# Key half of a KV compression by three products for even and odd chunks, with the turned rows copied whole to SBUF

## The reference, cut to what matters

```python
def compress_rows(rows, pe, w1, w2):          # once for keys, once for values
    ch = rows[:, :n_chunks * 16].reshape(B, n_chunks, 16, G, D)
    proj = jnp.einsum('bnsgd,psdh->pbngh', ch, w1)      # p = 0, 1: two taps
    h = proj[0, :, 0:n_blk] + bias[0]
    h = h + proj[1, :, 1:1 + n_blk] + bias[1]
    return jnp.einsum('bngh,hd->bngd', jax.nn.silu(h), w2)
```

## Time and profile before

| | us |
|---|---|
| timed, median of three runs | 2232.06 (2231.8, 2232.06, 2240.67) |
| span of the profiled execution | 2233.0 |
| paged steps of the stage, 370 to 971 | 601 |
| PE busy, whole span | 2092.5 |

### The profile page before, as it was taken

The page is one execution under the profiler, slowest core; times in us unless marked ns, Lnnn a source line. Parts: engine busy times, 40 slices in busy tenths (PEclk is TensorE's granted clock), DMA queues, the critical chain, the costliest instruction groups (busy, mean ns, idle before and its releaser), DMA issues. The chain is left out here.

```text
span 2233.0 us, 41102 instructions
## 1 busy us (share of the span) xinstructions
PE 2092.5 (94%) x16006; PEld 1877.4 (84%) x16006; DVE 1471.5 (66%) x3233; ACT 1004.9 (45%) x2112; POOL 607.8 (27%) x932
## 2 busy tenths in 40 slices
PE   6999999999999999996789898997999999999997
PEld 5999997777777777774678787777999999999997
DVE  4222225777776776786578687558688788765667
ACT  4114223655554664654367486325333333334334
POOL 0001003444443443431069596120111111110000
PEclk9999999999999999986879999998999999999999
DMA  4116565554654654658510011331332332365342
GB/s 128 57 57 186 191 224 168 194 196 163 201 171 133 212 167 149 177 137 276 191 52 8 8 48 48 108 109 41 101 114 75 101 116 77 97 239 193 118 165 97
DMA packets 217338, 295.53 MB, mean 132 GB/s; under 512 B 23474, under 2 KB 160914, under 8 KB 207762
## 3 DMA queue, kind: packets, MB, share of 16 engines
q1 hardware_dynamic: 199736, 191.64, 27.7%
q0 software_dynamic: 17408, 101.26, 13.0%
HBM read 217.12 MB, written 82.63 MB: 134 GB/s over the span
## 5 line engine op out<-in xcount | busy, mean ns | idle before, releaser
L3241 DVE TENSOR_TENSOR a_XTL<-cpt,a_XTH 64x256 fp32r<-64x256 f32 (+1 forms) x576 | 230.5, 400 | 87.9 <-ACT a_XTH L3126 79.5
L3126 ACT CAST a_XTH<-cpt 64x256 fp32r<-64x256 f32 (+1 forms) x576 | 201.4, 350 | 97.5 <-PE cpt L3350 85.3
L3365 PE MATMUL cph<-a_XTH,w1H 128*128 128x512 f32 x512 | 216.0, 422 | 0.0
L3365 PE MATMUL cph<-a_XTL,w1H 128*128 128x512 f32 x512 | 204.4, 399 | 0.0
L3365 PE MATMUL cph<-a_XTH,w1L 128*128 128x512 f32 x512 | 204.1, 399 | 0.0
L1558 POOL TENSOR_TENSOR C<-C,a_mt 128x264 f32<-128x264 f32 x66 | 69.0, 1064 | 404.9 <-ACT C L1643 269.9
L2077 PE MATMUL f<-a_slot,wd_slot 128*128 128x264 f32 x1176 | 148.2, 285 | 2.0 <-DVE a_slot L1887 1.4
L2077 PEld LDWEIGHTS f<-a_slot,wd_slot 128*128 128x128 f32 x1176 | 144.8, 188 | 3.0 <-issue 2.2
L2040 PE MATMUL f<-a_b,ring 128*128 128x264 f32 x1056 | 144.0, 286 | 3.3 <-DVE a_b L1783 2.7
L2040 PEld LDWEIGHTS f<-a_b,ring 128*128 128x128 f32 x1056 | 135.5, 190 | 3.8 <-issue 3.8
L492 PE MATMUL pj<-wH,xL 128*128 128x256 f32 (+2 forms) x464 | 130.9, 282 | 0.0
(11 more groups left out here) (582 smaller groups left out, 5560.7 us busy)
## 6 DMA issues: line engine op xcount, KB each, us to landing
a_slot<-a_T SPq DMA_DIRECT2D x20, 792.0 KB, 4.6
raw<-in_w_in POOLq DMA_DIRECT2D x12, 1024.0 KB
V<-v_s SPq DMA_DIRECT2D x6, 2048.0 KB, 10.3
v_s<-X SPq DMA_DIRECT2D x22, 512.0 KB, 6.0
raw<-in_w_gate SPq DMA_DIRECT2D x22, 512.0 KB, 5.2
raw_odd<-in_w_val SPq DMA_DIRECT2D x22, 512.0 KB, 6.1
a_T<-C SPq DMA_DIRECT2D x20, 528.0 KB, 3.3
a_T<-sums SPq DMA_DIRECT2D x11, 792.0 KB, 4.9
```

Of the source, the lines that this page charges most:

```text
L3126: nc.scalar.copy(turned(XTH, u, s, k, g, a), split(bank(at, k)[:], u, k, g, a)).then_inc(h_ready, 1)
L3241: last = nc.vector.tensor_tensor(turned(XTL, u, s, k, g, a), split(bank(at, k)[:], u, k, g, a), hi.bitcast(F32), ALU.subtract)
L3365: last = nc.tensor.matmul(out[:, :, 0:n], w[:, s, k, q, m * P:(m + 1) * P], x[:, s % 2, k, :, q:q + n], **flags)
```

## The change

For the key half, the 256 chunks are split in even ones E and odd ones O, 128 of each for each head. A block at an even position is w0·E + w1·O of the same pair, a block at an odd position w0·O + w1·E of the next pair. The kernel computes three products: w0·O and w1·E (kept apart in the banks `taps`), and (w0 + w1)·(E + O) in the bank `joint`; the even blocks are the joint product less the two others, the odd ones their sum with a shift of one. Each is of 256 columns (two heads by 128), so a step takes 2 x 2 x 3 + 2 x 3 = 18 matmuls of 256 columns. The values half keeps both taps on all chunks, in 24 matmuls of 256 columns, in two parts of twelve.

The turned rows of both halves are copied by ACT from PSUM to SBUF (`raw_copy`, four pieces of 64x256 for a half); the split into high and low part then runs from SBUF in one operation of 128x512 on ACT and one on DVE for a half. The sum E + O and its split are further operations of 128x256. There is one bank `cpt` for all turnings. At a unit's end ACT copies `taps` to SBUF (`keep_taps`), DVE joins them (`join_taps`), and Silu runs there in place. The sum of the taps, `wsum`, is made on DVE in `project_in` (L94), its split at the stage's start (`low_taps`). X has four slots of two token positions, gathered by two transfers of 4 KB rows in every step, three steps ahead; `values` stores once a step. The prompt's rows have a place of their own (`XP`) and are loaded in eight transfers during the last unit. `kvc` has one buffer. As pages now lie over the partitions in another order, `page`, `idx`, `c_overlap`, `c_part` and the index into V and the block maxima in `select` (L2155) are changed to fit.

The diff, cut to its core:

```diff
+        raws = [sb("raw", [P, 512])[:], prow[:].rearrange("p k n -> p (k n)")]
-        pt = [ctx.enter_context(nc.psum_tensor(f"cpt{i}", [P, 512], F32)) for i in range(2)]
+        pt = ctx.enter_context(nc.psum_tensor("cpt", [P, 512], F32))
         def turn_free(eng, at, kind):
...
+            if kind == 0 and 1 <= at <= PAIRS:
+                eng.wait_ge(kt_ready, at)
+            elif kind == 0 and at > PAIRS:
+                eng.wait_ge(l_ready[1], at)
+            elif kind and at < PAIRS:
+                eng.wait_ge(raw_ready[kind - 1], at + 1)
+            elif kind == 1:
+                eng.wait_ge(l_ready[0], at + 1)
...
             for at in range(LAST):
+                if at + 3 < PAIRS:
+                    gather(at + 3)
                 if at % 2 == 0:
-                    if at // 2 + 3 < TILES:
-                        gather(at // 2 + 3)
...
+            def keep_taps(u):
+                act.wait_ge(mm_ready[0], NS * u + NS)
...
+                for m in range(2):
+                    nc.scalar.copy(hs[:, 0, m].rearrange("p g n -> p (g n)"), taps[m][:]).then_inc(taps_kept, 1)
...
+            def raw_copy(at, k):
                 act.wait_ge(t_ready[k], at + 1)
+                if at >= 1:
+                    act.wait_ge(l_ready[k], at)
+                for g, a in parts:
+                    last = nc.scalar.copy(part_of(raws[k], at, g, a), split(at, g, a))
+                last.then_inc(raw_ready[k], 1)
+            def high_part(at, k):
...
+                    nc.scalar.copy(XH[:, at % 2, k, :], raws[k]).then_inc(h_ready[k], 1)
...
+            def high_sum(at):
+                act.wait_ge(sum_ready, at + 1)
+                nc.scalar.copy(SH[:, at % 2, :], raw[:, 0:256]).then_inc(sumH_ready, 1)
...
+            def high_parts(at, between=None):
+                if at < PAIRS:
+                    raw_copy(at, 0)
+                if at < LAST:
+                    high_part(at, 0)
+                if between:
+                    between()
+                if at < PAIRS:
+                    raw_copy(at, 1)
+                if at < LAST:
+                    high_part(at, 1)
+                if at < PAIRS:
+                    high_sum(at)
+                    keys_high(at)
...
                 if at % 2 == 0 and 2 <= at <= PAIRS:
                     keep_scores(at // 2 - 1)
+                high_parts(at + 1, (lambda: keep_taps(u)) if s == NS - 1 and u < DB else None)
...
+            def low_part(at, k):
+                dve.wait_ge(h_ready[k], at + 1)
...
+                elif k == 1:
+                    nc.vector.tensor_tensor(XL[:, at % 2, 1, :], raws[1], XH[:, at % 2, 1, :].bitcast(F32), ALU.subtract).then_inc(l_ready[1], 1)
+                else:
+                    lows(nc.vector.tensor_tensor(XL[:, at % 2, 0, :], raw, XH[:, at % 2, 0, :].bitcast(F32), ALU.subtract))
+                    nc.vector.tensor_tensor(raw[:, 0:256], raw[:, 0:256], raw[:, 256:512], ALU.add).then_inc(sum_ready, 1)
+            def low_sum(at):
+                dve.wait_ge(sumH_ready, at + 1)
+                nc.vector.tensor_tensor(SL[:, at % 2, :], raw[:, 0:256], SH[:, at % 2, :].bitcast(F32), ALU.subtract).then_inc(l_ready[0], 1)
...
+            def low_taps(s, n):
+                dve.wait_ge(wsH_ready, n)
+                nc.vector.tensor_tensor(ws[:, s, 1, :], keep["wsum"][:, s, :], ws[:, s, 0, :].bitcast(F32), ALU.subtract).then_inc(ws_ready, 1)
+            def join_taps(u):
+                for m in range(2):
+                    dve.wait_ge(taps_kept, 2 * u + m + 1)
+                    dve.wait_ge(even_ready, 2 * u + m)
+                    x = hs[:, 0, m]
+                    boths(nc.vector.tensor_tensor(both[:], x[:, :, 0:P], x[:, :, P:2 * P], ALU.add))
+                    boths(nc.vector.tensor_tensor(x[:, :, P:2 * P - 1], x[:, :, 0:P - 1], x[:, :, P + 1:2 * P], ALU.add))
+                    nc.vector.tensor_tensor(x[:, :, 0:P], joint[:, 256 * m:256 * m + 256].rearrange("p (g n) -> p g n", g=NG), both[:], ALU.subtract
+                                            ).then_inc(even_ready, 1)
...
+            low_part(0, 1)
+            low_sum(0)
+            low_taps(slice(0, 1), 1)
             keys(0)
+            low_taps(slice(1, NS), 2)
             dve.wait_ge(row_ready, 1)
...
+            def project_first(at):
...
+                    for q, y in ((0, O), (1, E)):
+                        for part, (w, x) in three(w1H[:, s, 0, q, rows], w1L[:, s, 0, q, rows], XH[:, at % 2, 0, y], XL[:, at % 2, 0, y]):
+                            nc.tensor.matmul(out[:, :, q, :], w, x, start=(begins and q + part == 0), stop=(ends and q == 1 and part == 2),
...
+                    for part, (w, x) in three(ws[:, s, 0, rows], ws[:, s, 1, rows], SH[:, at % 2, :], SL[:, at % 2, :]):
+                        last = nc.tensor.matmul(joint[:, 256 * m:256 * m + 256], w, x, start=(begins and m + part == 0),
...
+            def project_second(at, m):
+                pe.wait_ge(l_ready[1], at + 1)
...
                 turn(at + 1, 0)
-                project(at, 0)
+                project_first(at)
                 if u >= 1 and s == 4:
                     blocks(u - 1)
                 turn(at + 1, 1)
                 if chunk and n >= 1:
                     wide_products(n)
                     small_products(n, (0, 1))
-                project(at, 1)
+                project_second(at, 0)
+                score(at)
+                turn(at + 1, 2)
                 if chunk and n >= 1:
                     small_products(n, (2, 3))
-                turn(at + 1, 2)
-                score(at)
+                project_second(at, 1)
```

More of the change, by code:

```diff
@@ L3351, in turn @@
[L3351 to L3353 removed]
+                if at >= LAST or (kind == 2 and at >= PAIRS):
+                    return
+                if kind == 0 and at < PAIRS:
+                    pe.wait_ge(x_in[at % SLOTS], 32 * (at // SLOTS + 1))
+                elif kind == 0:
+                    pe.wait_ge(xp_in[at % 4], 16 * ((at - PAIRS) // 4 + 1))
+                turn_free(pe, at, kind)
+                if at >= PAIRS:
+                    for a in range(2):
+                        last = nc.tensor.transpose(pt[:, P * a:P * a + NCP], XP[0:NCP, at - PAIRS, a, P * kind:P * kind + P], ident[0:NCP, 0:NCP])
+                else:
+                    for h in range(2):
+                        for a in range(2):
+                            c = P * (2 * h + a if kind < 2 else 2 * a + h)
+                            last = nc.tensor.transpose(pt[:, c:c + P], X[:, at % SLOTS, h, a, P * kind:P * kind + P], ident[:])
@@ new lines, in turn, with project_prompt @@
+                last.then_inc(t_ready[kind], 1)
+            three = lambda wH, wL, xH, xL: enumerate(((wH, xH), (wL, xH), (wH, xL)))
+            def project_prompt(at, k):
+                s = at % NS
+                x = lambda X2, q: X2[:, at % 2, k, q:q + P]
+                w = lambda w2, q: w2[:, s, k, q, :]
+                for q in range(2):
+                    for part, (v, y) in three(w(w1H, q), w(w1L, q), x(XH, q), x(XL, q)):
+                        last = nc.tensor.matmul((taps, plain)[k][0][:, 0:256], y, v, start=(s + q + part == 0),
+                                                stop=(s == NS - 1 and q == 1 and part == 2))
+                last.then_inc(mm_ready[k], 1)
@@ L3368, in project @@
-                last.then_inc(mm_ready, 1)
+                    pe.wait_ge(hs_ready[1], u)
+                if u == DB:
+                    if m == 1:
+                        project_prompt(at, 1)
+                    return
+                begins, ends = s == 0, s == NS - 1
+                rows = slice(m * P, m * P + P)
+                out = plain[m][:].rearrange("p (g h n) -> p h g n", g=NG, h=2)
+                for q, h, c in ((0, 0, 0), (0, 1, 256), (1, 0, 256), (1, 1, 1)):
+                    for part, (w, x) in three(w1H[:, s, 1, q, rows], w1L[:, s, 1, q, rows], XH[:, at % 2, 1, c:c + 256], XL[:, at % 2, 1, c:c + 256]):
+                        last = nc.tensor.matmul(out[:, h], w, x, start=(begins and q + h + part == 0), stop=(ends and q + h == 2 and part == 2),
+                                                skip_group_check=True)
```

395 lines of the change are left out of this document (196 added, 199 removed).

## The result

The changed kernel takes 2316.51 us (median; 2314.28 to 2317.62) where the kernel before takes 2235.18 in the same runs: a ratio of 1.0366, interval 1.0346 to 1.0386. It is slower by 81 us; the forecast was 2289, slower by 57, and its range ended at 2330.

A forecast was written before the change was run, and what follows sets the result against it. PE was taken to bound the paged steps. 2233.0 - 36 + 48.3 + 4.8 + 22 + 2.7 + 11 + 4 = 2289.8, less 0.9: 2289 us; the forecast's own range was 2255 to 2330, the overall range 2245 to 2330.

The forecast's parts named there:

- The wait that is added: Paged even steps: PE's second turning waits for ACT's raw copy, 2.3 us in 21 steps, +48.3.
- Rival 2: Paged steps: PE stays the bound in every step, no stall and no clock fall, 2214 us; chance 0.11.
- Rival 4: Half-width matmuls don't take half the time, or gain and stall cancel: within 0.5%, 2221 to 2243; chance 0.07.
- PE's own work: 64 paged steps: fewer matmul columns save PE 0.56 us a step, -36 in all if PE stays the bound.
- The clock: Behind the paged steps' stalls the granted clock falls, 14 times 1.6 us, +22; bounds 0 and 49.
- Rival 1: Paged even steps: the stall comes but the clock does not fall, 2267 us; chance 0.31.
- The unit's end: Last step of each of eight units: keep_taps and join_taps add 0.6 us a unit, +4.8; bounds 0 and 26.
- Start: Stage start: low_taps subtracts on DVE ahead of a_brow, for which PE waits, +2.7; bounds 0 and 5.2.
- Prompt unit: Its eight steps: with one bank the second half's turning waits for the first half's subtractions, 1.4 us each, +11.
- Operands from SBUF: Paged steps: DVE operations with both operands in SBUF are held up beside GpSimd, +4; bounds 0 and 33.
- rival 3: Paged stage: GpSimd shuts out DVE's SBUF operations in every step, 2318 us; chance 0.05.

The follow-up runs named there:

- e7_before_raw: The kernel before with only ACT's raw copies and the 128x512 split from SBUF added, two turning banks and all matmuls kept: 2264.77 us, ratio 1.0126.
- e11_before_raw_sq: e7_before_raw with ACT's squares moved behind the next even step's first half: 2233.23 us, ratio 0.9984 to the kernel before.
- e5_all: The changed kernel with squares behind the first raw copy, joint as second prompt-unit bank, and most of low_taps, half of join_taps and Silu moved later: 2229.41 us.
- e8_prompt_bank: The changed kernel with squares behind the first raw copy and joint as second turning bank in the prompt unit: 2228.43 us, ratio 0.9961 to the kernel before.

## Why the prediction was right, and where it was off

**The wait that is added.** Right in place, link by link and nearly in size: 22 waits of 2.5, 54.9 us, where 21 of 2.3, 48.3, were forecast. The place that was not counted is s = 4 of unit 0, which has no `blocks` to cover the wait. Taking one link out (scores) took 1.2 from each wait, taking the earlier one out (squares) took the wait. Rival 2, PE staying the bound, falls: the chain begins at the third turning, and DVE's relief does not shorten it (`weigh` still took 2.3). Rival 4 falls by the matmuls' 1.51 and by the time itself. That the squares' wait costs nothing in the kernel before was not quite right: the control, which moves them there, is 8 us faster.

**PE's own work.** 0.56 a step was forecast, 0.63 came in odd steps. If all 64 steps had it, -40.

**The clock.** The mechanism was right, two waits of the same 2.4 with and without a fall included; the size was a little low: 22 against some 26 by the rate above. The mean granted clock is below 1.00 in 15 of the 22 steps that wait, where 14 were taken. That two guesses of two thirds came so near is luck, as no row before had such a wait. Rival 1 falls with the falls of the clock.

**The unit's end.** Mis-sized: 0.6 a unit was taken on top of an odd step, and 1.7 came (9.2 for 7.5), 13 us in all. `join_taps` stands ahead of `keys` on DVE, and the turning of the next step waits for these keys, 8.0 us in 7 places. The prediction counted the operations' 2.0 us as covered by an odd step's slack, which DVE's order did not give. PE then waits twice, 1.2 for the keys and 2.7 for the raw copy, and s = 0 has the lowest granted clock, 0.76 in four units.

**Start.** 5.1 for 2.7, at the upper bound. The row shows what stands ahead of `brow`:

```profile
370.74 2.02 DVE L3308 TENSOR_TENSOR ws<-X,ws 128x1792 fp32r<-128x1792 f32 x1 [0.89 <-ACT ws L3189]
372.68 0.40 DVE L3350 COPY a_brow<-chg 2x256 f32<-2x256 f32 x1
```

The subtraction is 2.02, and ACT's conversion ahead of it is in series too, 0.89. These make 2.9 of the 5.1. The third turning already starts 1.3 later (367.89 for 366.55), and the eight matmuls on `brow` last 0.8 more from start to the next turning (1.79 for 0.98), at a granted clock of 0.50.

**Prompt unit.** Forecast +11. From its first turning to its `blocks` it grew from 49.4 to 60.9, +11.5, and the second bank gave 9 back.

**Operands from SBUF.** Charged at 4, and not to be seen in the change:

```profile
L3295 DVE TENSOR_TENSOR a_XL<-a_raw,a_XH x64: 675/692/890, 358.9 to 1018.9; 128x512 fp32r<-128x512 f32 x64
```

The longest is 0.89, and the change's three other operations of this kind stay at or below 0.70, so rival 3 falls here. The shut-out that the Trainium skill describes ("SBUF — State Buffer", section "Who interferes with whom") does exist, as the 4.93 us in `e7_before_raw` agree. Its length differs: by that section whoever issues first has the shared ports for the whole instruction, and 26 of the 39 subtractions over 1 us in `e7_before_raw` and `e11_before_raw_sq` (1.2 to 2.0 us) do end with the GpSimd operation that they met, but nine stood through ten or more in a row. Why some wait out a run is open.

**What was left out of the sum.** The step terms as measured or estimated, -40 + 55 + 26 + 13, make 54 of the 56.7 us; some 3 us of the paged steps have no row of their own. The 7.6 us behind the stage are mostly in the prompt's attention, whose code did not change. It lasted 286.9 before and 293.6 after, but also 293.9 in `e5_all` and 286.8 in `e8_prompt_bank`, with granted clocks of 0.93, 0.89, 0.90 and 0.93: it takes one or the other time in kernels with the same code there, and why is open.

Against the profile's 82.8 the forecast of 57 was thus too small by 26 (by 24 against the medians): 8.6 of the units' ends, 7.6 behind the stage, 6.6 of the waits, 4 of the clock, 2.4 each at the start and in the prompt unit with what follows it, and the 3 without a row, less 4 each of PE's work and of the operands from SBUF, which came out better.

## What to carry to other kernels

When a change takes a buffer away, walk back from the instruction that empties the one that is left, along its engine's program order: an instruction of 0.3 us that waits for another engine cost 8 us here as long as a second buffer covered it, and 79 when none did. Work taken off the bounding engine is worth its time only in those steps where that engine still bounds; before crediting a gain to the change, try the mended order on the kernel before, which here was as fast without it.

## What the hardware showed that was not expected

A DVE subtraction of 128x512 with both operands in SBUF, 0.69 us alone, was held for 4.93 and up to 5.31 us, through a run of some fifteen GpSimd operations, while most of the others that were held waited for one. And PE given 2.1 us of useless matmuls in each of its waits ended 21 us earlier, with the granted clock up (0.98 for 0.94).
